# Four weight chunks of each gated feed-forward, computed as seven quarter products

## The reference, cut to what matters

```
def swiglu(u, w_in, w_out):                      # u 256x1024, w_in 1024x5632, w_out 2816x1024
    gate, up = jnp.split(u @ w_in, 2, axis=-1)
    return (jax.nn.silu(gate) * up) @ w_out

for l in range(2):
    x = x + 0.5 * rmsnorm(swiglu(rmsnorm(x, g1), ffn1_w_in[l], ffn1_w_out[l]), g2)
    x = x + rmsnorm(hybrid_mixer(rmsnorm(x, g3), ...), g4)
    x = x + 0.5 * rmsnorm(swiglu(rmsnorm(x, g5), ffn2_w_in[l], ffn2_w_out[l]), g6)
```

## Time and profile before

| what | us |
|---|---|
| median of three timed runs | 2336.15 (2336.0 to 2336.83) |
| span of the profiled execution, first to last instruction | 2333.0 |
| TensorE matmul busy | 2310.1, 99% of the span |
| VectorE busy | 1526.0, 65% |
| ScalarE busy | 1226.6, 53% |
| DMA | 434.90 MB, mean 186 GB/s |

### The profile page before, as it was taken

One profiled execution on the slowest core, in us unless ns is written; L12 is line 12 of the kernel. 1 busy time (PEld: TensorE's weight loads), 2 busy tenths in 40 slices (PEclk: granted clock), 3 DMA queues, 4 the chain that ended last, 5 costly groups with the idle time before them and its releaser, 6 DMA issues.

```text
span 2333.0 us, 30308 instructions
## 1 busy us (share of the span) xinstructions
PE 2310.1 (99%) x12100; PEld 1954.5 (84%) x12100; DVE 1526.0 (65%) x1987; ACT 1226.6 (53%) x1788; POOL 72.5 (3%) x134
## 2 busy tenths in 40 slices
PE   8999999999999999999999999999999999999998
PEld 6888887888888888978888888888889788888887
DVE  6867567776566666865575665665667665756664
ACT  6555446554455556745444554555567453445553
POOL 0110000100000000000000000000000000000000
PEclk9999999999999999999999999999999999999999
DMA  8436656356656556645565465565566455554653
GB/s 298 142 118 225 213 172 223 123 165 215 208 166 212 187 178 195 205 154 182 182 195 197 154 210 198 178 218 188 172 195 211 154 180 182 190 197 162 198 192 125
DMA packets 119803, 434.90 MB, mean 186 GB/s; under 512 B 13552, under 2 KB 13808, under 8 KB 119664
## 3 DMA queue, kind: packets, MB, share of 16 engines
q1 hardware_dynamic: 119664, 432.96, 56.2%
HBM read 431.86 MB, written 1.05 MB: 186 GB/s over the span
## 4 chain that ended last, share of the span: by engine, by line
PE 91%; DVE 5%; ACT 1%; DMA 1%; POOL 1%; issue 1%; SPq 0%; DVEq 0%; POOLq 0%; ACTq 0%
PE ub L1659 22%; PE ub L1663 11%; PE ub L1637 9%; PE ub L1639 8%; PE ub L1638 8%; PE acc L1637 8%; PE acc L1639 8%; PE acc L1638 8%; DVE wlo L992 1%; PE ub L1644 1%; PE ub L1645 1%; PE ub L1646 1%; DMA raw<-in_w 1%; DVE XN L1033 1%; ACT junk L528 1%
## 5 line engine op out<-in xcount | busy, mean ns | idle before, releaser
L992 DVE TENSOR_TENSOR wlo<-raw,whi 128x1024 fp32r<-128x1024 f32 x776 | 915.9, 1221 | 257.4 <-ACT whi L506 255.3
L506 ACT ACTIVATE whi<-raw 128x1024 fp32r<-128x1024 f32 x776 | 783.1, 1053 | 255.6 <-PE ub L1639 145.7
L1659 PE MATMUL ub<-xhl,whi 128*128 128x512 f32 x2176 | 595.2, 395 | 0.0
L1659 PEld LDWEIGHTS ub<-xhl,whi 128*128 128x128 f32 x2176 | 375.5, 189 | 54.6 <-issue 2.3
L1663 PEld LDWEIGHTS ub<-xhl,wlo 128*128 128x128 f32 x2176 | 333.5, 189 | 45.9
L1663 PE MATMUL ub<-xhl,wlo 128*128 128x256 f32 x2176 | 346.0, 281 | 0.0
L1637 PE MATMUL acc<-whi,bhl 128*128 128x512 f32 x736 | 288.4, 392 | 0.0
L1639 PE MATMUL acc<-whi,bhl 128*128 128x512 f32 x736 | 287.6, 391 | 0.0
L1638 PE MATMUL acc<-wlo,bhl 128*128 128x512 f32 x736 | 287.4, 391 | 0.0
L1637 PE MATMUL ub<-whi,xhl 128*128 128x512 f32 (+1 forms) x704 | 275.4, 391 | 5.2 <-DVE wlo L992 3.7
L1639 PE MATMUL ub<-whi,xhl 128*128 128x512 f32 (+1 forms) x704 | 272.8, 388 | 0.0
(11 more groups left out here) (302 smaller groups left out, 2440.6 us busy)
## 6 DMA issues: line engine op xcount, KB each, us to landing
raw<-in_w SPq DMA_DIRECT2D x776, 512.0 KB, 4.9
gain<-in_gains SPq DMA_DIRECT2D x20, 512.0 KB, 8.0
tapw<-in_taps SPq DMA_DIRECT2D x16, 512.0 KB, 4.4
DEC<-in_decay SPq DMA_DIRECT2D x2, 768.0 KB, 7.6
par<-in_par SPq DMA_DIRECT2D x2, 647.0 KB, 7.5
par<-in_par SPq DMA_DIRECT2D x2, 556.0 KB, 7.7
H<-in_x SPq DMA_DIRECT2D x2, 512.0 KB, 4.3
out_h<-H SPq DMA_DIRECT2D x4, 256.0 KB, 2.6
```

The costliest lines, as they stand in the source:

```text
L506: do(act.activation(whi[:, s % RING, c], raw[:, s % RAW, c], ACT.Copy), counts["w_hi"])
L992: do(dve.tensor_tensor(wlo[:, s % RING, c], raw[:, s % RAW, c], whi[:, s % RING, c].bitcast(f32), ALU.subtract), counts["w_lo"])
L1659: pe.matmul(bank, whi[:, s % RING, n:n + P], xhl[:, kt, :, :].rearrange("p a n -> p (a n)"), start=kt == 0, stop=False, skip_group_check=True)
```

## The change

In each gated feed-forward the chunks up 10 to up 13 (units 10 to 13 and their gates) are replaced by one block with seven products. The input is taken as a 2 x 2 matrix of quarters (two halves of the tokens by two halves of the width), and so are the weights (two halves of the width by 512 gate columns and 512 value columns). The Winograd form of Strassen's scheme needs seven products of quarters in place of eight: four with sums of the input and four with sums of the weights. Each quarter of the weights is one chunk of 128 x 2048, used with 128 tokens: 12 matmuls of 512 columns.

- Order: after up 9 come b11, t1, t3, t2, b22, b21, t4, then up 14, up 15, and then down j and up 16+j by turns, for j from 0 to 5, then the downs 6 to 10. `FFN2_OPS` is 36 places of the stream with 33 loads.
- `RAW` goes from 2 to 4 slots. `places()` works out beforehand which slot each load takes and after which `lo` it may start. A quarter stays in its slot until its last use.
- Every product has its own split: `prep` and `lo` run for all seven. The four weight sums are subtractions of VectorE in `raw` itself, two halves each (`weight_sums`, called by `lo` when the second half of b11, t1 and t2 is split).
- The four input sums are made by VectorE during up 4 to 7 (`input_sum`, ten operations on 128 x 512), ScalarE makes their high parts during up 5 to 8, VectorE the rests (`s_ready`) during up 6 to 9.
- Product t1 waits for all four `s_ready`. VectorE and ScalarE combine the products in SBUF, and TensorE transposes the result behind up 14.
- The DMA scratch area shrinks from 16640 bytes to 1280, which makes room; the memset of `XA`'s pads is done in each layer, since `UB` lies over `XA`.

```diff
-RAW = 2
+RAW = 4
+SCRATCH = 1024
+PRODUCTS = ("b11", "t1", "t3", "t2", "b22", "b21", "t4")
+QUARTERS = ("b11", "b12", "b22", "b21")
+SUMS_AFTER = dict(b11=(("t1", "b12", "b11"), ("t3", "b22", "b12")), t1=(("t2", "b22", "b11"),), t2=(("t4", "b21", "b11"),))
+X_SUMS = dict(t1=0, t2=1, t3=2, b22=3)
+X_SUM_ORDER = (0, 1, 3, 2)
 def ffn2_order():
     seq = [("first", j) for j in range(4)] + [("up", j) for j in range(4, 10)]
+    seq += [("prod", n) for n in range(len(PRODUCTS))] + [("up", 14), ("up", 15)]
     for j in range(6):
-        seq += [("down", j), ("up", 10 + 2 * j), ("up", 11 + 2 * j)]
+        seq += [("down", j), ("up", 16 + j)]
     return seq + [("down", j) for j in range(6, 11)]
...
# SyncE, load(s)
+                    if LOADS[s] is None:
+                        return
+                    chunk, slot, until = LOADS[s]
...
+                        if until >= 0:
+                            sp.wait_ge(sem["w_lo"], 2 * until + k + 1)
...
# ScalarE, ffn
+                                elif 5 <= j <= 8:
+                                    i = X_SUM_ORDER[j - 5]
+                                    nxt("s_sum")
+                                    do(act.activation(sxh[:, 4 * i:4 * i + 4, :], quad(UB[:, i, :]), ACT.Copy), counts["s_hi"])
...
+                            elif kind == "prod":
+                                prep(s + 3)
+                                if j == 0:
+                                    used(s)
+                                    act.wait_ge(sem["s_ready"], 4 * (m - 2) + 4)
+                                    do(act.activation(UB[:, 0, :], acc[:, 0, :], ACT.Copy), counts["st_act"])
+                                elif j == 3:
+                                    used(s)
+                                    do(act.activation(UB[:, 1, :], acc[:, 0, :], ACT.Copy), counts["st_act"])
+                                elif j >= 5:
+                                    act.wait_ge(sem["st_dve"], 5 * (m - 2) + j - 3)
+                                    x = UB[:, 8 - j, :]
+                                    do(act.activation(x, x, ACT.Silu), counts["st_g"])
...
# VectorE, behind lo of both halves of a product's weights
+                def weight_sums(s0, behind):
+                    slot, nth = quarters_of(s0)
+                    for _, plus, minus in SUMS_AFTER.get(behind, ()):
+                        settle()
+                        for k in range(2):
+                            c = slice(k * HALF, (k + 1) * HALF)
+                            dve.wait_ge(sem[f"w_in{2 * slot[plus] + k}"], 16 * nth[plus])
+                            do(dve.tensor_tensor(raw[:, slot[minus], c], raw[:, slot[plus], c], raw[:, slot[minus], c],
+                                                 ALU.subtract), counts["summed"])
...
# VectorE, ffn
+                                if 4 <= j <= 7:
+                                    input_sum(j - 4)
+                                if 6 <= j <= 9:
+                                    i = X_SUM_ORDER[j - 6]
+                                    nxt("s_hi")
+                                    do(dve.tensor_tensor(sxl[:, 4 * i:4 * i + 4, :], quad(UB[:, i, :]),
+                                                         sxh[:, 4 * i:4 * i + 4, :].bitcast(f32), ALU.subtract), counts["s_ready"])
...
+                            elif kind == "prod":
+                                u = m - 2
+                                if j == 4:
+                                    dve.wait_ge(sem["st_act"], 2 * u + 2)
+                                    do(dve.tensor_tensor(UB[:, 2, :], UB[:, 1, :], acc[:, 1, :], ALU.add), counts["st_dve"])
+                                    settle()
+                                    do(dve.tensor_tensor(UB[:, 3, :], UB[:, 2, :], acc[:, 2, :], ALU.add), counts["st_dve"])
+                                elif j == 5:
+                                    used(s - 1)
+                                    settle()
+                                    do(dve.tensor_tensor(UB[:, 2, :], UB[:, 2, :], acc[:, 3, :], ALU.add), counts["st_dve"])
+                                elif j == 6:
+                                    used(s - 1)
+                                    do(dve.tensor_tensor(FH[:, 0, :], UB[:, 0, :], acc[:, 0, :], ALU.add), counts["st_dve"])
+                                lo(s + 3)
+                                if j == 6:
+                                    dve.wait_ge(sem["st_g"], 2 * u + 2)
+                                    settle()
+                                    do(dve.tensor_tensor(FH[:, 0, :], FH[:, 0, :], UB[:, 2, :], ALU.mult), counts["st_fh"])
+                                    used(s)
+                                    do(dve.tensor_tensor(FH[:, 1, :], UB[:, 1, :], acc[:, 2, :], ALU.add), counts["st_dve"])
+                                    settle()
+                                    do(dve.tensor_tensor(FH[:, 1, :], FH[:, 1, :], UB[:, 3, :], ALU.mult), counts["st_fh"])
...
# TensorE
+                def product(u, s, name):
+                    if name == "t1":
+                        pe.wait_ge(sem["s_ready"], 4 * u + 4)
...
+                    A_[n].take(pe, sem[event], value)
+                    for k in range(4):
+                        arrive(s, k // 2)
...
+                        last = wide_tile(acc[:, n, :], x_h, x_l, s, k * 512, name not in ("t2", "t4") and k == 0, k == 3)
+                    give(last)
+                def turn_unit(u, hid):
+                    for t in range(2):
+                        pe.wait_ge(sem["st_fh"], 2 * u + t + 1)
+                        A_[t].take(pe, sem["hid"], hid + t)
+                        for q in range(4):
+                            last = pe.transpose(acc[:, t, q * P:(q + 1) * P], FH[:, t, q * P:(q + 1) * P], ident)
+                        give(last, "tr_done")
```

More of the change, by code:

```diff
@@ L75, with places, load, quarters_of @@
 AT2 = {key: n for n, key in enumerate(ORDER2)}
+B2 = dict(end=len(ORDER2))
 FFN_AT = {(0, "f1"): 2, (0, "f2"): 3, (1, "f1"): 4, (1, "f2"): 5}
+FFN2_OPS = len(ffn2_order())
+def places():
+    free, came = [-1] * RAW, [0] * RAW
+    lies, loads, chunk, made = [], [], 0, 0
+    quarter = {}
+    def load(until):
+        nonlocal chunk
+        slot = min(range(RAW), key=lambda n: free[n])
+        loads.append((chunk, slot, free[slot]))
+        chunk += 1
+        came[slot] += 1
+        free[slot] = until
+        return slot, came[slot]
+    for s, key in enumerate([("", 0)] * (LAYERS * B1["end"]) + ORDER2 * LAYERS):
+        if not key[0].endswith("prod"):
+            lies.append((*load(s), None))
+            continue
+        n, name = key[1], PRODUCTS[key[1]]
+        if n < len(QUARTERS):
+            q = QUARTERS[n]
+            quarter[q] = load(s - n + PRODUCTS.index(DONE_WITH[q]))
+        else:
+            loads.append(None)
+        slot, count = quarter[LIES_IN[name]]
+        if name[0] == "b":
+            lies.append((slot, count, None))
+        else:
+            lies.append((slot, 0, made + SUM_ORDER.index(name)))
+        if n == len(PRODUCTS) - 1:
+            made += len(SUM_ORDER)
+    return lies, loads
+LIES, LOADS = places()
+def quarters_of(s0):
+    got = {q: LOADS[s0 + n][1] for n, q in enumerate(QUARTERS)}
+    nth = {q: sum(1 for x in LOADS[:s0 + n + 1] if x and x[1] == got[q]) for n, q in enumerate(QUARTERS)}
+    return got, nth
+UNITS_AT = [s for s, key in enumerate([("", 0)] * (LAYERS * B1["end"]) + ORDER2 * LAYERS)
+            if key[0].endswith("prod") and key[1] == 0]
 P1 = dict(conv_b=0, ln_g=4, ln_b=8, pool_scale=12, conv_pw=14, pool_w=1038, end=1294)
@@ L129, in build @@
     with ExitStack() as ctx:
-        place = [16640]
+        place = [SCRATCH + 256]
         def sb(name, units, dtype=f32, at=None, shape=None):
@@ L253, in build @@
                  "root_ready coef_ready has xs sd md sigs exd va oq ro sm2 pv2 rp rph rx sc2 mh mx mixed par_free "
-                 "va_done fa fg fp fr").split()
+                 "va_done fa fg fp fr summed s_sum s_hi s_ready st_act st_dve st_g st_fh").split()
         sem = {n: ctx.enter_context(nc.semaphore(n)) for n in names}
@@ L504, in prep @@
                         c = slice(k * HALF, (k + 1) * HALF)
-                        act.wait_ge(sem[f"w_in{n % (2 * RAW)}"], 16 * (n // (2 * RAW) + 1))
-                        do(act.activation(whi[:, s % RING, c], raw[:, s % RAW, c], ACT.Copy), counts["w_hi"])
+                        slot, came, made = LIES[s]
+                        if made is None:
+                            act.wait_ge(sem[f"w_in{2 * slot + k}"], 16 * came)
+                        else:
+                            act.wait_ge(sem["summed"], 2 * made + k + 1)
+                        do(act.activation(whi[:, s % RING, c], raw[:, slot, c], ACT.Copy), counts["w_hi"])
                         at[0] += 1
@@ L981, in _ @@
```

(11 more changed lines are left out.)

96 lines of the change are left out of this document (71 added, 25 removed).

## The result

The changed kernel takes 2393.14 us (2392.57 to 2394.19, four runs) against 2336.07 (2335.95 to 2336.83) for the kernel before: a ratio of 1.0242, interval 1.0230 to 1.0254. The profiled execution has a span of 2390.8 us against 2333.0, so 57.8 us are to be found.

A forecast was written before the change was run, and what follows sets the result against it. TensorE, with matmuls in flight for 99% of the span, was taken as the bound. 4 x (15.1 delay + 0.5 clock) - 2 for slots = +60 us, span 2393, timed 2396 us; range 2383 to 2414, or 2374 to 2420 with rivals.

The forecast's parts named there:

- TensorE's arithmetic: Seven products and eight transposes replace four up chunks: -2.2 us per feed-forward, -9 us for four, if nothing waits.
- VectorE's queue: From the start of up 4: old work 30.5, input sums 9.1, weight sums 7.0, together 46.6 us; `s_ready` at 763.4.
- The wait: TensorE stands idle before product t1 until `s_ready` is complete: 15.7 us in each of four feed-forwards.
- Behind the wait: After t1 starts, VectorE needs 23.4 us, to 786.8; TensorE ends the block at 787.3, a delay of 15.1 us.
- The clock: First matmuls after each wait may run at half speed: 0.5 us net taken, bounds 0 to 2.6.
- Four slots: Four raw load slots let loads start two chunks earlier, anywhere in the kernel: 2 us gained, at most 3.7.
- The sum: Four feed-forwards of 15.1 us delay and 0.5 for the clock, less 2 for the slots: +60 us.
- The total from the span: Timed runs were taken to lie 3.0 to 3.8 us above the span, so span 2393 gave 2396 us.
- VectorE's idle third covering it: Rival: spare VectorE time in up 4 to 9 absorbs the sums, 2325 us; turning point about 6 us; chance 0.06.
- half of it hiding: Rival: VectorE's waits for ScalarE vanish when late, leaving about 8 us per feed-forward: +30, 2366 us; chance 0.09.
- the low clock for the whole block: Rival: six products at 0.43 us per matmul, 28 us per feed-forward, 2449 us; chance 0.06.
- VectorE gap-free from up 5: Sign expected in the profile after: VectorE's queue without gaps from up 5 to the last product.

The follow-up runs named there:

- e10: Changed kernel without input sums and weight sums, with the end of the combination ahead of the split of down 0: 2328.61 us, ratio 0.9967.
- e1: Changed kernel without its four weight sums, products taking raw quarters of the weights: 2366.3 us, ratio 1.0127 to the kernel before.
- e5: Changed kernel with 58 extra matmuls keeping TensorE busy ahead of t1's wait, nothing left out: 2387.53 us, ratio 1.0222.
- e4: Kernel before with four raw slots and the smaller DMA scratch alone: 2335.25 us, ratio 0.9997.
- e2: Changed kernel without input sums, their high parts and rests, products taking raw quarters of the input: 2362.0 us, ratio 1.0112.
- e6: Changed kernel with the input sums moved earlier, to the four "first" chunks, nothing left out: 2362.5 us, ratio 1.0115.
- e7: Changed kernel with the weight sums on GpSimd instead of VectorE, nothing left out: 2412.91 us, ratio 1.0330.

## Why the prediction was right, step by step

- **TensorE's arithmetic**, -2.2 us for each feed-forward: measured -2.17 (e10). Right, though one reading was off: up 5's start of 716.52 is that of the chain, and down 0's of 744.37 that of the timeline, on which up 5 starts at 716.28. An up chunk takes 5.60 us and not 5.57.
- **VectorE's queue**, 46.6 us from the start of up 4, `s_ready` at 763.4: in the kernel after the queue starts at 717.19 and ends at 762.33, so 45.1. The terms for the sums are borne out (7.2 us of wait less without 7.0 of weight sums, e1). The sums take 9.1 and 7.0 us in the rows too. The 1.5 us too many lie in the old work, 29.1 us where I had counted 30.5: an up whose split stands behind other work takes 4.2 to 4.5 us without the sums, not 4.62. The waits for `whi`, 0.26 in an up before, vanish once VectorE is late, and more than the "up to 1 us" that I had left to the range went. In the chain above the split of 750.70 follows its addition of 750.02 without one.
- **The wait**, 15.7 us in each of four: measured 14.6, each at the first matmul of t1, released by `sxl`. Right in place, number and cause; too long by the same term.
- **Behind the wait**, `FH` at 786.8 and the block's end at 787.3: `FH` at 785.46 (the last multiply starts at 784.77 and takes 0.69) and the end at 786.94, in a trace whose second stack starts 0.4 us later than before. From the start of t1 VectorE took 23.1 us, and I had 23.4. The wait for `FH`, 1.4 us in the forecast, is not there: at the low clock TensorE comes to the transposes only at 786.15. Up 9 was to start 0.6 us late; the rows show less than 0.1 (its first matmul is at 739.24, up 8's last run of four is at 738.73 and such a run is followed after 0.47).
- **The clock**, 0.5 us in each block, from bounds of 0 to 2.6 net: measured 2.0 on TensorE by the rows (8.0 in four), 1.4 net by e5's medians. That it would fall was right, and the 2 to 4 us that I had put on TensorE hold at their low end. Too small was the net: I had said that 1.4 would lie in the wait for `FH`, and without the low clock that wait is 0.5 us (e5).
- **Four slots**, -2 us: nothing (e4). I bounded the gain by TensorE's waits for `wlo` and took the middle, without asking whether those waits came from memory.
- **The sum**, +60: the trace has 58.3 us of waits, 8.0 of low clock and -8.7 of arithmetic, 57.6 of the 57.8 between the spans; the medians are 57.1 apart. For each block the forecast had 15.6 (15.1 and 0.5), and a quarter of 57.8 is 14.5. The wait was put too long by 1.1, up 9's lateness by 0.5 and the wait for `FH` by 1.4, against 1.5 too little for the clock and 0.4 to 0.5 too little for the arithmetic, since half of the transposes had been laid under that wait. Four times 1.1 too much and the 2 us of the slots too little leave 2.4 in the span. So the forecast was closer than its terms, and part of that is luck.
- **The total from the span**: I had added 3.0 to 3.8 us to the span. The changed kernel's profiled execution took 2392.59 us with a span of 2390.8, so 1.8 lie around it. The kernel before has the same, 1.7 to 1.8 us, in the executions for which both are on record (2335.56 us with a span of 2333.8, for one). The 3.0 to 3.8 came from setting its timed runs against the span of another, somewhat faster execution.
- **The rivals.** VectorE's idle third covering it, half of it hiding, and the low clock for the whole block are all refuted by the same rows: 14.6 us of wait with 12.7 of 14 us busy, and the 2.4 GHz level again after 8 to 11 matmuls of t1's 12 (from 766 on in the first block). The first rival's turning point was too high as well: 16.1 us of additions give 14.6 of wait, the 9.1 of e1 give 7.4, so some 1.6 us are covered, and by this estimate the change would break even at about 3.8 us ahead of `s_ready` (1.6 and the 2.17 gained, the clock not counted), not at 6. No run lies there, and e2 and e6 lose 26 us with no wait for `s_ready` at all, behind it.
- **VectorE gap-free from up 5**: nearly. From the addition of up 4 to the last rest it is busy for 41.3 of 45.1 us, and what is missing is mostly the 0.48 us in each up in which it waits for ScalarE's copy of the unit (`bhl`), which in turn needs VectorE's product:

```profile
717.19:762.33 45.14, 30.62 (x172) 26.30 (x170) 41.29 (x54) 23.94 (x38) 0.00 (x0) 0.89 0.32 107
```

What stays open: sums of weights that take no VectorE time at this place (made by the DMA engines, in another part of the kernel with more room, or with signs by which fewer sums are needed) were not tried.

## What to carry to other kernels

An idle share says nothing about a place: add up the queue of the helping engine from a point where it is in step to the first thing that the bound engine waits for, and charge whatever exceeds the bound engine's own work there in full. Seven products for eight bought 2.17 us of TensorE with 9.4 us of weight sums and some 9 of input sums; the input sums could be moved to where they were free, the weight sums, which must follow the weights' arrival, found no such place in these runs. And behind one long wait there are others of the same queue that appear only when it is gone, so price the second before counting the first as a gain.

## What the runs showed that I had not expected

- GpSimd beside VectorE: a half of 128 x 1024 in float32 takes GpSimd 2.9 to 3.0 us, and VectorE's operations with two SBUF operands take 2.06 to 2.82 us instead of 0.42 to 0.69 while it runs. Moving eight halves in each block, 1.2 us each on VectorE, to an engine that was 97% idle made the kernel slower by 20 us (e7 against the kernel after).
- The price of a long wait on TensorE's clock is small: after 14.6 us of idleness 8 to 11 matmuls at the 1.2 GHz level, 1.7 to 2.3 us, and then 2.4 GHz again. It does not grow with the wait in these runs: behind waits of 7.4 us (e1) 11 to 13 matmuls were slow, and behind waits of 2.7 us (e2) 7 to 14. So a short wait can cost as much in clock as a long one.
- Twice as many load slots took ScalarE's waits for loads from 94 us to 11 (e4) and changed the time by nothing that can be measured.
